# A two-block network in one launch: three steps of the SSD and GLA scan put in another order on GpSimd, ScalarE and VectorE

## The reference

```python
def ssd_gla_layer(x, ...):
    h = rms_norm_2(x, norm_w)
    u = h @ w_in
    z_a, xbc, dt_raw, q_b, k_b, v_b, gate_lr, g_b = split_cols(u, EVEN_SPLITS)
    xbc = silu(causal_depthwise_conv(xbc, conv_w, conv_b))
    xs, bm, cm = split_cols(xbc, ...)
    dt = softplus(dt_raw + dt_bias)
    y_a = ssd_chunked_scan(xs, dt, a, bm, cm, d)          # 16 heads of 64
    y_a = rms_norm_2(y_a * silu(z_a), ssd_norm_w)
    log_decay = log_sigmoid(gate_lr @ gate_w2 + gate_b) / 16
    o_b = gla_chunked(q_b, k_b, v_b, log_decay)           # 8 heads, values of 128
    o_b = rms_norm_2(o_b, gla_norm_w).reshape(...) * silu(g_b)
    return x + concatenate([y_a, o_b]) @ w_out
```

## Time and profile before

| | |
|---|---|
| median of 3 runs | 840.57 us (840.34 to 841.18) |
| the profiled execution | 840.04 us |
| its span in the trace | 838.2 us |
| TensorE's granted clock | 0.999 |
| busy: TensorE | 828.9 us (99%) |
| busy: VectorE | 623.1 us (74%) |
| busy: ScalarE | 505.2 us (60%) |
| busy: GpSimd | 124.2 us (15%) |

### The profile page before, as it was taken

The page is one execution under the profiler, slowest core; times in us unless marked ns, Lnnn a source line. Parts: engine busy times, 40 slices in busy tenths (PEclk is TensorE's granted clock), DMA queues, the critical chain, the costliest instruction groups (busy, mean ns, idle before and its releaser), DMA issues.

```text
span 838.2 us, 16865 instructions
## 1 busy us (share of the span) xinstructions
PE 828.9 (99%) x6768; PEld 799.4 (95%) x6768; DVE 623.1 (74%) x1055; ACT 505.2 (60%) x877; POOL 124.2 (15%) x119
## 2 busy tenths in 40 slices
PE   9999999999999999999999999999999999999997
PEld 8999999999999999999999999999999999888896
DVE  6657888886666689777664478999889696568765
ACT  7447566555444576555554368787978554356755
POOL 1000000000000305433441100043515010000002
PEclk9999999999999999999999999999999999999999
DMA  9754334445555536655665535645555376654331
GB/s 320 264 159 143 134 114 164 127 146 180 178 184 192 170 101 202 206 178 184 194 193 187 195 90 164 193 139 181 162 162 175 102 231 187 187 173 129 127 101 51
DMA packets 39854, 139.81 MB, mean 167 GB/s; under 512 B 4433, under 2 KB 5089, under 8 KB 39649
## 3 DMA queue, kind: packets, MB, share of 16 engines
q1 hardware_dynamic: 38160, 135.90, 50.9%
q10 hardware_dynamic: 1616, 2.84, 1.1%
HBM read 137.65 MB, written 1.06 MB: 165 GB/s over the span
## 4 chain that ended last, share of the span: by engine, by line
PE 88%; DVE 6%; ACT 3%; issue 1%; POOL 1%; DMA 0%; DVEq 0%; SPq 0%; ACTq 0%; POOLq 0%
PE ps L1806 66%; PE ps L1871 4%; PE ps L1809 4%; PE ps L1830 4%; DVE weights_lo L1076 2%; PE ps L2006 1%; PE ps L1991 1%; PE ps L2020 1%; PE ps L2275 1%; PE ps L2293 1%; DVE arena L1386 1%; PE ps L1927 1%; ACT weights_hi L543 1%; PE ps L2283 1%; PE ps L2135 1%
## 5 line engine op out<-in xcount | busy, mean ns | idle before, releaser
L1076 DVE TENSOR_TENSOR weights_lo<-raw_weights,weights_hi 128x1024 fp32r<-128x1024 f32 x251 | 312.3, 1248 | 83.2 <-ACT weights_hi L543 82.0
L543 ACT ACTIVATE weights_hi<-raw_weights 128x1024 fp32r<-128x1024 f32 x250 | 262.2, 1053 | 145.5 <-PE ps L1806 61.1
L1806 PE MATMUL ps<-x_hi,weights_hi 128*128 128x256 f32 (+3 forms) x1184 | 341.8, 289 | 0.3 <-DVE weights_lo L1076 0.2
L1806 PE MATMUL ps<-x_lo,weights_hi 128*128 128x256 f32 (+3 forms) x1184 | 333.7, 282 | 0.0
L1806 PE MATMUL ps<-x_hi,weights_lo 128*128 128x256 f32 (+3 forms) x1184 | 333.0, 281 | 0.0
L1806 PEld LDWEIGHTS ps<-x_hi,weights_hi 128*128 128x128 f32 x1184 | 222.8, 188 | 6.8 <-issue 5.6
L1806 PEld LDWEIGHTS ps<-x_lo,weights_hi 128*128 128x128 f32 x1184 | 222.9, 188 | 0.6 <-issue 0.4
L1806 PEld LDWEIGHTS ps<-x_hi,weights_lo 128*128 128x128 f32 x1184 | 223.2, 189 | 0.0
L1806 PE MATMUL ps<-y_hi,weights_hi 128*128 128x256 f32 (+1 forms) x488 | 137.7, 282 | 0.0
L1806 PE MATMUL ps<-y_lo,weights_hi 128*128 128x256 f32 (+1 forms) x488 | 137.4, 282 | 0.0
L1806 PE MATMUL ps<-y_hi,weights_lo 128*128 128x256 f32 (+1 forms) x488 | 137.1, 281 | 0.0
(11 more groups left out here) (280 smaller groups left out, 1185.9 us busy)
## 6 DMA issues: line engine op xcount, KB each, us to landing
raw_weights<-weights_in SPq DMA_DIRECT2D x251, 512.0 KB, 4.0
arena<-decay_rows ACTq DMA_DIRECT2D x8, 256.0 KB, 4.0
masks<-masks_in SPq DMA_DIRECT2D x1, 1186.0 KB, 8.4
raw_weights<-weights_in SPq DMA_DIRECT2D x4, 256.0 KB, 4.4
hidden<-xT_in SPq DMA_DIRECT2D x3, 272.0 KB, 5.0
hidden<-xT_in SPq DMA_DIRECT2D x1, 276.0 KB, 3.1
gate_w<-gate_w_in ACTq DMA_DIRECT2D x1, 256.0 KB, 3.7
out<-arena ACTq DMA_DIRECT2D x1, 256.0 KB, 2.1
```

Of the source, the lines that this page charges most:

```text
L543: a.sig(A(whi[:, s * CW:(s + 1) * CW], raw[:, (c % RAW) * CW:(c % RAW + 1) * CW], ACT.Copy), "hi_ready")
L1076: d.sig(TT(wlo[:, s * CW:(s + 1) * CW], raw[:, (c % RAW) * CW:(c % RAW + 1) * CW], whi[:, s * CW:(s + 1) * CW].bitcast(F32), ALU.subtract) ...
L1806: ins = mm(bank(BANK_OF[no])[:, 0:b - a], wt, x_[:, kt, a:b], start=s0, stop=s1)
```

## The change

Three steps are moved; no instruction is added or taken away.

1. GpSimd, p = 1: the weights of u = 3 (heads 6 and 7) stand ahead of the sum of squares of u = 1. For p = 2 and 3 the sum stays ahead.
2. ScalarE, p = 2 and 3: the norm factor of the GLA pair of the round before (`gla_rms(p - 1)`) stands ahead of the copies of this round's values (`take_values(p)`).
3. VectorE, p = 2 and 3: the norm itself (`gla_norm(p - 1)`) stands ahead of the half of the gate of u (`z_half(("ez", u), ...)`).

```diff
@@ -508,8 +508,11 @@
                 ssd_weights(2 * p)
                 gla_keys(p)
                 gla_products(p)
-                ssd_add(2 * p - 1)
+                if p > 1:
+                    ssd_add(2 * p - 1)
                 ssd_weights(2 * p + 1)
+                if p == 1:
+                    ssd_add(1)
                 ssd_add(2 * p)
             ssd_add(KT - 1)
@@ -945,8 +948,8 @@
                     if p == 3:
                         gla_squares(2)
                     feed(("ev", p))
+                    gla_rms(p - 1)
                     take_values(p)
-                    gla_rms(p - 1)
                     feed(("ez", u))
                     half_tanh(("ez", u), zs[:, 0, :])
                     decays(u + 1)
@@ -1592,8 +1595,8 @@
                     feed(("ek", p))
                     ssd_y(u)
                     feed(("ev", p))
+                    gla_norm(p - 1)
                     z_half(("ez", u), zs[:, 0, :])
-                    gla_norm(p - 1)
                     feed(("ez", u))
                     ssd_args(u + 1)
                 z_half(("eg", u), gs[:, u % 4, :])
```

## The result

| | before | changed |
|---|---|---|
| median of 22 runs each | 840.23 us (839.90 to 841.61) | 841.50 us (840.91 to 842.09) |
| ratio | | 1.0013 (95%: 1.0007 to 1.0019) |
| profiled execution | 840.04 us | 841.23 us |
| span | 838.2 us | 839.4 us |

What follows compares the result with a forecast made beforehand. TensorE was taken as the bound, busy 828.9 of 838.2 us, with VectorE close behind it. The terms −0.1 + 0 + 0.1 + 0 sum to 0.0 on the median of 840.57: forecast 840.6 us, range 838.6 to 842.3.

Steps and rivals of the forecast that it cites:

- Its own signs: Trace signs: pair u=3 takes 0.8 us, TensorE waits near 583, both engines within 0.5 us of old places by 600.
- B: VectorE's z product, behind the norm, delays tanh and heads: 0.75 at p=2, 0.5 at p=3, up to 842.3; chance 0.12.
- The reading of the earlier trace: From 574 to 583 VectorE is busy 8.89 of 9 us, so TensorE could be only 0.36 us earlier.
- Edit 1, the stall goes: TensorE's pair u=3: GpSimd's weights end by 569.7 to 570.6, ahead of 571.22, so the 1.48 us stall goes.
- Edit 1, "TensorE then meets it ... about 0.16 earlier than now": At 583.31 VectorE is 0.2 later, TensorE 0.16 earlier; kernel's end taken −0.1, bounds −1.48 to +0.5 us.
- the gap of 0.36: From VectorE's copy of the GLA scores at 582.95 to TensorE's matmul at 583.31: the most TensorE can keep.
- Edit 2, 0: ScalarE, p=2 and 3: norm 0.81 us earlier, copies 2.67 later but hidden by 18.7 us; taken 0.
- Edit 3 at p=2, +0.1: VectorE's z product behind the norm moves ScalarE's tanh by 0.3 to 0.75; bounds −0.69 and +0.75, taken +0.1 us.
- Edit 3 at p=3, 0, hidden with 0.2 to spare: VectorE's norm uses 0.58 us of idle, z product ends at 637.2, tanh stays at 637.42; bounds 0 and +0.5.
- A: VectorE's products shrink by 1.16 at u=3, so TensorE keeps all 1.48: 839.1, or 838.4 with p=2's 0.69; chance 0.18.
- C: At u=3 VectorE stands still for whole GpSimd instructions: 1.64 later, TensorE 1.28 later at 583.31, 842.0 us; chance 0.08.
- D: The GpSimd move does nothing, since the weights at u=3 are still not done at 571.22: 840.6 us; chance 0.02.

Runs made afterwards that it cites:

- e1: Only GpSimd's weights of u=3 moved ahead of the sum of squares, against the kernel before: 841.05 us against 840.29, ratio 1.0009.
- e2: Only ScalarE's norm factor moved ahead of the value copies at p=2 and 3, against the kernel before: 840.34 us against 840.29, ratio 1.0001.
- e3: ScalarE's and VectorE's moves at p=2 and 3 without GpSimd's, against the kernel before: 840.88 us against 840.29, ratio 1.0007.
- e6: ScalarE's and VectorE's moves at p=3 alone, without GpSimd's, against the kernel before: 840.65 us against 840.37, ratio 1.0002.
- e4: GpSimd's move, with weights of heads 6 and 7 on only 8 of 384 columns, against the kernel before: 839.20 us against 840.29.

## Why the prediction held, and where its steps did not

The time lies inside the range and within 0.2%, but two terms of the sum were too small, and that the forecast held is owed to its width: the sum said 0.0, the change measured 1.1 us, and 0.2% is 1.7 us. Its own signs hold up to 583 and fail behind that. By 600 both engines were 0.62 us off their old places, not within 0.5. The tanh came 1.41 us later at p=2 and 1.17 at p=3, not 0.3 to 0.75 later and where it was. And the pair u=7 lost 1.88 us, clearly more than 0.96, which was to make B right.

- *The reading of the earlier trace rows:* wrong. The 8.89 us stand in the column of PEld, TensorE's loads of weights; VectorE is busy 8.40 of the 9 us. What was concluded from it held all the same: the 0.60 us of gaps took up nothing, and VectorE was as late at the copy of the scores as at 574.
- *Edit 1, the stall goes:* right. The pair u=3 starts at 571.17 and takes 0.88, and the wait comes back at 583, behind VectorE.
- *Edit 1, "TensorE then meets it ... about 0.16 earlier than now", taken −0.1, at most +0.5:* wrong; e1 measured +0.65, outside the bounds. Two sizes were off. The gate products cost 1.56 more, not 0.81: the nearest row, 1.57 at p=3, was taken beside instructions of GpSimd of 0.7 to 0.8 us, the weights take 1.0. The split (+0.54, forecast +0.55) and the relief (1.25, forecast 1.16) were right; a further 0.26, from the next split, was not counted. VectorE's copy was 0.63 later, not 0.2. And the gap of 0.36 was used once: at 583.64 TensorE is 0.33 later, which is 0.63 less 0.30 of the gap; by u=4 it is 0.61 later, because the next split that TensorE meets leaves it almost no gap. Before, that split and TensorE's first matmul on it were:

```profile
589.86 1.22 DVE L1076 TENSOR_TENSOR weights_lo<-raw_weights,weights_hi 128x1024 fp32r<-128x1024 f32 x1
...
591.21 0.31 PE L1809 MATMUL ps<-weights_hi,x_hi 128*128 128x256 f32 x1
```

  From 589.86 + 1.22 = 591.08 to 591.21 are 0.13 us, where the changed kernel, which waits there, has 591.75 − 591.71 = 0.04: a gap of about 0.09, not of 0.36. So the prediction measured the gap at one meeting, and the narrowest one decides. The sentence that allowed for this ("VectorE's delay in full") was in the bounds, with VectorE's delay too small.
- *Edit 2, 0:* right, 0.06 in e2.
- *Edit 3 at p=2, +0.1:* the tanh moved by 603.76 − 603.01 = 0.75 in e3, the upper end of what was forecast, and the weights by 0.31; that they then escape VectorE's split was named and priced (−0.69), and measured −0.45. The forecast took the other end. What the step left out is that ScalarE and VectorE stay late by half a microsecond up to p=3.
- *Edit 3 at p=3, 0, hidden with 0.2 to spare:* right by itself (0.09 in e6, nothing to spare), wrong in the change, since ScalarE and VectorE arrive late there: 0.56 for both rounds. The prediction costed the two rounds each from the trace of before, as if the first left the second alone.
- *Rivals:* A, the stall's end carried through, needs a VectorE that GpSimd leaves alone; e4 shows it, at −0.97 instead of −1.48. B's mechanism, the z product as the late one at p=3, is what e3 shows, and its sign came in the changed kernel (1.88 at u=7); its price at p=2 was a gain, and its time, 842.3, did not come. C's full price (1.28) did not come: VectorE was 0.63 late. D falls: the weights end at 569.96, ahead of TensorE at 571.17. The Trainium skill (SBUF — State Buffer, Who interferes with whom) has a VectorE instruction with two SBUF inputs and a GpSimd instruction that reads SBUF contend for an exclusive port pair; e1 and e4 agree, 2.33 us with large weights and 0.78 with small ones for the same two instructions.

## What to carry to other kernels

A stall of TensorE is worth what the next engine behind it leaves free: look for the engine that has no gap in the same stretch, and cost the change by its end, since here three stalls of 0.7 to 1.5 us went away and the time did not fall. Look at every later place where TensorE meets another engine, not only at the first: here the end of the scan moved with the tanh of p=3 in nine of eleven runs. Moving work of GpSimd beside VectorE's short instructions with two SBUF inputs costs VectorE most of that work (1.62 of the 2.06 us of the two weights here, between e1 and e4). When one edit is made in two rounds, cost the second from where the first leaves the engines, not from the trace of before.

## What was not expected of the hardware

What VectorE loses beside GpSimd went, in these rows, by the number of instructions that meet, and not by their length: the two gate products of 0.4 us took 0.78 longer each (2.32 us instead of 0.76) beside the two weights of 1.0, and one split of 1.23 took 0.70 longer beside one weight (607.38 in e3). A GpSimd pair took 2.17 or 3.00 us by what VectorE happened to run. And executions of programs that are alike up to the scan reached its pair u=2 between 555.84 and 556.82 us, which is as much as the effects sought here; the late ones are those whose first transfer was long, as far as their chains show it (4.89 us in e2, 4.14 in before).
